# First two expert-query slots split by token halves inside the second norm, and three remainders made on Pool: one edit to a one-core decoder-layer kernel

## The reference, cut to what matters

```
h = layernorm(alpha * h + cross_attention(h))          # the "second norm"
q = h @ peer_wq          # 2048 x 2048: the expert queries
s = q . sub_keys         # per head and half, 128 keys; then top-16 and the experts
```

## Time and profile before

| | |
|---|---|
| time, median of 3 runs | 1891.31 us (1889.75 to 1891.76) |
| the profiled execution's own time | 1890.53 us |
| its span | 1888.8 us |
| PE busy | 98% of the span |
| DVE, ACT, POOL busy | 77%, 45%, 18% |
| the stretch of the change | from about 512 to 540 us of the span |

### The profile page before, as it was taken

One profiled execution on the slowest core, in us unless ns is written; L12 is line 12 of the kernel. 1 busy time (PEld: TensorE's weight loads), 2 busy tenths in 40 slices (PEclk: granted clock), 3 DMA queues, 4 the chain that ended last, 5 costly groups with the idle time before them and its releaser, 6 DMA issues.

```text
span 1888.8 us, 25810 instructions
## 1 busy us (share of the span) xinstructions
PE 1852.9 (98%) x10392; PEld 1625.5 (86%) x10392; DVE 1459.4 (77%) x1917; ACT 841.4 (45%) x1136; POOL 345.4 (18%) x216
## 2 busy tenths in 40 slices
PE   7999999999899999999999999999999999999997
PEld 6888888888688999999777889889889899898895
DVE  6544655576763798996888888888988988989886
ACT  5443456344533101223555545455455455454552
POOL 1000223000000001001333223222323223323200
PEclk9999999999989999999999999999999999999999
DMA  9645433746254777888999999999999999999881
GB/s 343 240 178 178 136 133 120 320 162 245 90 201 156 245 268 282 329 325 318 358 370 366 359 361 362 390 352 371 385 350 379 376 353 391 363 355 393 349 314 45
DMA packets 100199, 548.21 MB, mean 290 GB/s; under 512 B 8705, under 2 KB 33345, under 8 KB 35953
## 3 DMA queue, kind: packets, MB, share of 16 engines
q1 hardware_dynamic: 53424, 374.37, 52.2%
q0 software_dynamic: 20096, 147.04, 19.2%
q10 hardware_dynamic: 26560, 25.17, 4.3%
HBM read 530.74 MB, written 14.68 MB: 289 GB/s over the span
## 4 chain that ended last, share of the span: by engine, by line
PE 96%; DVE 1%; ACT 1%; DMA 1%; issue 1%; SPq 0%; POOL 0%; DVEq 0%; ACTq 0%
PE bank L947 15%; PE bank L849 11%; PE bank L575 11%; PE bank L592 9%; PE bank L949 7%; PE bank L880 6%; PE bank L883 6%; PE bank L881 6%; PE bank L879 6%; PE bank L882 6%; PE bank L577 5%; PE bank L869 2%; PE bank L815 1%; DMA ring_raw<-in_stream 1%; PE bank L682 0%
## 5 line engine op out<-in xcount | busy, mean ns | idle before, releaser
L575 PE MATMUL bank<-act_split,ring_hi 128*128 128x512 f32 x896 | 319.4, 400 | 10.9 <-DVE ring_lo L1355 8.2
L1816 DVE TENSOR_TENSOR split_a<-experts,split_a 128x2048 fp32r<-128x2048 f32 x120 | 274.6, 2289 | 53.1 <-ACT split_a L1270 52.8
L1344 DVE TENSOR_TENSOR ring_lo<-ring_raw,ring_hi 128x2048 fp32r<-128x2048 f32 x90 | 205.9, 2290 | 137.3 <-ACT ring_hi L1010 136.9
L1270 ACT CAST split_a<-experts 128x2048 fp32r<-128x2048 f32 x120 | 229.7, 1914 | 140.5 <-PE bank L883 139.7
L947 PE MATMUL bank<-h_split,split_a 128*128 128x384 f32 x944 | 270.8, 359 | 0.0
L577 PE MATMUL bank<-act_split,ring_lo 128*128 128x256 f32 x896 | 251.9, 281 | 0.0
L949 PE MATMUL bank<-h_split,split_a 128*128 128x192 f32 x944 | 236.3, 250 | 0.0
L549 POOL DMA_INDIRECT rows<-in_peer_u,eidx x64 | 139.9, 2186 | 448.9 <-DVE rows L1723 443.0
L549 POOL DMA_INDIRECT rows<-in_peer_v,eidx x64 | 153.0, 2391 | 368.4 <-DVE hrow L1729 344.7
L849 PE MATMUL bank<-h2T,experts 128*128 128x192 f32 x1280 | 216.3, 326 | 0.0
L575 PEld LDWEIGHTS bank<-act_split,ring_hi 128*128 128x128 f32 x896 | 169.7, 189 | 50.4 <-DVE act_split L1355 8.0
(11 more groups left out here) (277 smaller groups left out, 3422.5 us busy)
## 6 DMA issues: line engine op xcount, KB each, us to landing
experts<-in_stream SPq DMA_DIRECT2D x221, 1024.0 KB, 7.4
ring_raw<-in_stream SPq DMA_DIRECT2D x91, 1024.0 KB, 4.8
late_raw<-in_stream SPq DMA_DIRECT2D x35, 1024.0 KB, 7.9
gate_matrix<-stage ACTq DMA_DIRECT2D x12, 1024.0 KB, 4.9
gbuf<-gate_matrix ACTq DMA_DIRECT2D x16, 768.0 KB, 12.9
w<-in_w SPq DMA_DIRECT2D x4, 1024.0 KB, 8.7
gb<-in_ln_g POOLq DMA_DIRECT2D x3, 1024.0 KB, 4.8
gb<-in_ln_b POOLq DMA_DIRECT2D x3, 1024.0 KB, 9.2
```

The source lines that it names most:

```text
L575: pe.matmul(bank[n % 2][:, :], hi[:, k * P:(k + 1) * P], act_split[:, k].rearrange("p c t -> p (c t)"), start=(k == 0), stop=False, skip_g ...
L1270: act.copy(split(m)[0], tile).then_inc(split_hi, 1)
L1344: dve.tensor_tensor(ring_lo[:, r, :], ring_raw[:, r, :], ring_hi[:, r, :].bitcast(F32), ALU.subtract).then_inc(lo_ready, 1)
L1816: dve.tensor_tensor(lo, raw_slot(split_slot(m))[0], hi.bitcast(F32), ALU.subtract).then_inc(split_lo, 1)
```

## The change

Four edits, in one stretch.

1. PE: the first two query slots are done by token halves. `half_slot(b, t, q)` does 4 of the 16 `k` steps of slot b for the 128 tokens of half t: a matmul of 2 x 128 columns with the slot's high part and one of 128 columns with its low part. The order is: turn t=0, slots 0 and 1 for t=0, turn t=1, slots 0 and 1 for t=1, and then `block_slot` for the other 14 slots.
2. ACT: the four copies to the high part come first, and the whole copies to `h2T` after the low parts.
3. DVE: all four `half_low` of t=0 come before the first `scaled` of t=1, mixed with two `centred`, and the four of t=1 after the norm.
4. POOL makes the low parts of the second to fourth slot (three subtractions of 128 x 2048), which DVE made after its last `half_low`. The turned tiles go to other banks.

```diff
--- before.py
+++ after.py
@@ -520,6 +520,11 @@
                 for j, name in enumerate((f"ln{k + 1}_g", f"ln{k + 1}_b")):
                     pool.dma_start(gb[:, j, :], a[name].partition_broadcast(P)).then_inc(gb_landed, 16)
 
+            pool.wait_ge(lo_ready, S_PQ + 1)
+            for s in range(S_PQ + 1, S_PQ + R):
+                pool.wait_ge(hi_ready, s + 1)
+                pool.tensor_tensor(ring_lo[:, s % R, :], ring_raw[:, s % R, :], ring_hi[:, s % R, :].bitcast(F32),
+                                   ALU.subtract).then_inc(lo_ready, 1)
             pool.wait_ge(ln_ready, 16)
             pool.wait_ge(slots_done, S_PQ + 1)
             pool.dma_start(subk[:], a["subkT"]).then_inc(subk_landed, 16)
@@ -816,17 +821,49 @@
                                              ring[w][:, r, i * 512:(i + 1) * 512], start=(i == 0 and n == 0),
                                              stop=(i == 3 and n == 2))
                     last.then_inc(slots_done if t else xo_first, 1)
-            for t in range(TT):
+            def turn_half(t, q):
+                pe.wait_ge(ln_ready, 8 + 4 * t + q + 1)
+                if t and q >= 2:
+                    pe.wait_ge(act_lo, A_XO + q - 1)
+                    pe.wait_ge(h2_ready, q - 1)
+                for i in range(4):
+                    k = 4 * q + i
+                    last = pe.transpose(bank[PQ_BANKS[t][q]][:, i * P:(i + 1) * P], hres[:, t, k * P:(k + 1) * P], ident[:])
+                last.then_inc(ht_done, 1)
+            def half_slot(b, t, q):
+                out = bank[(N_PQ + b) % 2]
+                if q == 0 and t == 0:
+                    pe.wait_ge(lo_ready, S_PQ + b + 1)
+                    pe.wait_ge(dve_nb, 8 + 4 + XO_BANKS[1].index((N_PQ + b) % 2) + 1)
+                if b == 0:
+                    pe.wait_ge(act_lo, A_XO + 4 * t + q + 1)
+                hi, lo = (pq_first[:, w] if b == 0 else ring[w][:, (S_PQ + b) % R] for w in range(2))
+                tokens = slice(t * P, (t + 1) * P)
+                for k in range(4 * q, 4 * q + 4):
+                    pe.matmul(out[:].rearrange("p (c t) -> p c t", c=2)[:, :, tokens], hi[:, k * P:(k + 1) * P],
+                              act_split[:, k, :, tokens], start=(t == 0 and k == 0), stop=False, skip_group_check=True)
+                    last = pe.matmul(out[:, tokens], lo[:, k * P:(k + 1) * P], actT_hi[:, k, tokens], start=False,
+                                     stop=(k == KO - 1), skip_group_check=True)
+                if t and q == 3:
+                    last.then_inc(slots_done, 1)
+            for q in range(4):
+                turn_half(0, q)
+            for q in range(4):
+                half_slot(0, 0, q)
+            for q in range(4):
+                half_slot(1, 0, q)
+            for q in range(4):
+                turn_half(1, q)
+            for b in range(2):
                 for q in range(4):
-                    pe.wait_ge(ln_ready, 8 + 4 * t + q + 1)
-                    for i in range(4):
-                        k = 4 * q + i
-                        last = pe.transpose(bank[XO_BANKS[t][q]][:, i * P:(i + 1) * P], hres[:, t, k * P:(k + 1) * P], ident[:])
-                    last.then_inc(ht_done, 1)
-
-            for b in range(16):
+                    half_slot(b, 1, q)
+            for b in range(2, 16):
                 pe.wait_ge(tb_out, N_PQ + b - 1)
-                block_slot(S_PQ + b, N_PQ + b, fresh=[A_XO + n for n in HALF_LOW] if b == 0 else None)
+                block_slot(S_PQ + b, N_PQ + b)
 
             pe.wait_ge(tb_out, N_U)
             pe.wait_ge(dve_nb, 16)
@@ -1199,21 +1236,28 @@
             for b in range(1, 4):
                 high(S_PQ + b)
 
+            def turned(t, q):
+                return bank[PQ_BANKS[t][q]][:].rearrange("p (k t) -> p k t", k=4)
             def turned_high(t, q):
+                act.wait_ge(ht_done, 8 + 4 * t + q + 1)
+                act.copy(actT_hi[:, 4 * q:4 * q + 4, t * P:(t + 1) * P], turned(t, q)).then_inc(act_hi, 1)
+            def turned_whole(t, q):
                 n = (P, ND - P)[t]
-                act.wait_ge(ht_done, 8 + 4 * t + q + 1)
-                turned = bank[XO_BANKS[t][q]][:].rearrange("p (k t) -> p k t", k=4)
-                act.copy(actT_hi[:, 4 * q:4 * q + 4, t * P:(t + 1) * P], turned).then_inc(act_hi, 1)
-                act.copy(h2T[:, 4 * q:4 * q + 4, t * P:t * P + n], turned[:, :, 0:n]).then_inc(h2_ready, 1)
+                act.wait_ge(act_lo, A_XO + 4 * t + q + 1)
+                act.copy(h2T[:, 4 * q:4 * q + 4, t * P:t * P + n], turned(t, q)[:, :, 0:n]).then_inc(h2_ready, 1)
 
             act.wait_ge(slots_done, S_PQ)
-            turned_high(0, 0)
-            turned_high(0, 1)
+            for q in range(4):
+                turned_high(0, q)
             deviation(3, slice(1, 2))
-            turned_high(0, 2)
-            turned_high(0, 3)
+            for q in range(4):
+                turned_whole(0, q)
             for q in range(4):
                 turned_high(1, q)
+            for q in range(4):
+                turned_whole(1, q)
             for b in range(16):
                 if b and b + AHEAD < 16:
                     high(S_PQ + b + AHEAD)
@@ -1648,10 +1692,9 @@
             def half_low(t, q):
 
                 dve.wait_ge(act_hi, A_XO + 4 * t + q + 1)
-                dve.wait_ge(h2_ready, 4 * t + q + 1)
                 sl = (slice(None), slice(4 * q, 4 * q + 4), slice(t * P, (t + 1) * P))
                 part((actT_hi[sl], actT_lo[sl]),
-                     bank[XO_BANKS[t][q]][:].rearrange("p (k t) -> p k t", k=4)).then_inc(act_lo, 1)
+                     bank[PQ_BANKS[t][q]][:].rearrange("p (k t) -> p k t", k=4)).then_inc(act_lo, 1)
 
             low(S_XO + 3)
             add_half(0, 0)
@@ -1668,24 +1711,20 @@
                     marks.append(centred(0, j + 2, gb))
             for j in range(1, NQ):
                 add_half(1, j)
+            half_low(0, 0)
             half_variance(1)
-            half_low(0, 0)
             half_low(0, 1)
-            marks = [centred(1, j, gb) for j in range(2)]
-            scaled(1, 0, gb, marks[0], 3)
+            marks = [centred(1, 0, gb)]
             half_low(0, 2)
-            scaled(1, 1, gb, marks[1], 3)
-            marks.append(centred(1, 2, gb))
-            half_low(1, 0)
-            scaled(1, 2, gb, marks[2], 3)
-            marks.append(centred(1, 3, gb))
-            half_low(1, 1)
-            scaled(1, 3, gb, marks[3], 3)
+            marks.append(centred(1, 1, gb))
             half_low(0, 3)
-            half_low(1, 2)
-            half_low(1, 3)
-            for b in range(1, R):
-                low(S_PQ + b)
+            for j in range(NQ):
+                scaled(1, j, gb, marks[j], 3)
+                if j + 2 < NQ:
+                    marks.append(centred(1, j + 2, gb))
+            for q in range(4):
+                half_low(1, q)
+            dve.wait_ge(lo_ready, S_PQ + R)
             for b in range(16):
                 block_sum(N_PQ + b, pq[:, b, :])
                 if b + R < 16:
@@ -1927,7 +1966,7 @@
 HT_BANKS = ((6, 7), (2, 3))
 HEAD_QUARTERS = (0, 2, 1, 3)
 XO_BANKS = ((2, 3, 4, 5), (1, 0, 6, 7))
-HALF_LOW = (4, 5, 7, 8)
+PQ_BANKS = ((2, 3, 4, 5), (6, 7, 2, 3))
 V0_BANKS = (2, 3, 0, 1)
 V0_FIRST = (0, 1, 2, 3)
 V0_LAST = (3, 2, 0, 1)
```

## The result

The changed kernel takes 1896.42 us (median of 8 runs, 1894.77 to 1898.31), the kernel before 1891.2 in the same comparison (8 runs, 1887.35 to 1892.6): a ratio of 1.0027, 95% interval 1.0018 to 1.0036. It is **slower by 0.27%**, 5.2 us. The forecast of 1885.8 had the wrong sign; the rival "DVE waits behind POOL" named 1898. The stated range, 1884.2 to 1897.5, holds 1896.42 only because it was drawn around gain and loss.

The account below looks back on a forecast made before the run. PE, busy for 98% of the span, was taken as the bound. Slot 2 5.6 us earlier, carried in full from 1890.5, gives 1884.9; with 0.8 for the median 1885.7, stated as 1885.8, range 1884.2 to 1897.5.

Parts of the forecast that it names:

- DVE waits behind POOL: Rival: `scaled` operations of t=0 wait for POOL's subtractions, DVE 10.8 us late, 6.7 us slower overall, 1898; chance 0.30.
- POOL's three subtractions: Slots 1 to 3's low parts on POOL: 5.4 us each, 7.0 available, so no cost if engines don't hamper each other.
- The rest (clock, less gaps): Rival's term for PE's long gap: 2.7 us lost to the clock's fall less 1.2 of gaps, 1.5 us.
- The time of 1896: The POOL-wait rival reckoned with 4497 ns per POOL operation instead of 5.4 us: DVE delay 9, time 1896.
- The half steps: PE's steps in slots 0 and 1 by token halves: 0.225 us each, bounds 0.173 and 0.28.
- PE's new timeline: PE from turning t=0 to slot 2: slot 2 starts at 533.9 instead of 539.54, 5.6 us earlier.
- DVE's order: DVE's reordered low parts and norm: quarters may start from 516.2, norm of t=1 done at 524.0 instead of 525.1.
- DVE's three `ring_lo`: DVE's three subtractions, 6.7 us, lay under slot 0; without the move to POOL they would be a cost.
- ACT's order: ACT's same eight casts and eight copies in another order: costs nothing.
- Carrying it to the end: Slots 2 to 15 and the rest are PE's chain, so the 5.6 us gain reaches the end in full.
- the second rival: Clock falls in PE's gaps (1 to 2.5 us) or half steps are dear (3 us): about 1888; chance 0.14.
- dear half steps: Case in slots 0 and 1: half steps take 0.28 us each, costing 3 us of the gain.

Follow-up runs that it names:

- pool_timed: Changed kernel with POOL's first subtraction after the norm of t=0, the others after that of t=1, DVE's wait after the first block sum: 1888.03 us.
- pool_alone: Kernel before the change with only POOL's three subtractions moved over from DVE, whole slots kept: 1900.62 us.
- pool_memset: Changed kernel with POOL's three subtractions replaced by memsets to zero, so POOL only writes: 1887.83 us.
- pool_one_input: Changed kernel with POOL's three subtractions replaced by a one-input multiplication by zero in the same places: 1896.13 us.
- lows_on_dve: Changed kernel with POOL's three subtractions given back to DVE, behind its last low parts of t=0 and t=1: 1887.64 us.
- pool_timed_again: The kernel pool_timed unchanged, run once more for a second profile: 1888.34 us.
- pool_alone_timed: Kernel pool_alone with POOL's subtractions held back until the norm of t=1 is done, DVE's wait behind the first block sum: 1891.82 us.
- before: The kernel without the change, the reference: 1891.2 us.
- experiment 8: Changed kernel with each of POOL's three subtractions cut into eight pieces of 128 x 256, in the same places: 1890.39 us.
- after: The changed kernel with all four edits, against the kernel before: 1896.42 us.
- after_again: The changed kernel unchanged, run once more for a second profile: 1896.27 us.

## Why the prediction was wrong

**The step that failed** is that of POOL's three subtractions: "this costs nothing if the engines don't hamper each other". They do, and its price is the whole of the loss: 8.6 us of DVE, where the sum had 0. Take that hold away and the same work gains (pool_timed). The rows at hand said both things. Rows 8 showed POOL shut out for a whole operation by a DVE subtraction, and the Trainium skill ("SBUF — State Buffer", Who interferes with whom) says that the order of issue decides which of the two is blocked; rows 9 showed an overlap without it, and I gave rows 9 the greater weight. Rows 9 had operations of 128 and 256 columns with one input; the change has 2048 columns and two. pool_alone, pool_timed and pool_memset show that the exclusion is there at this size and that POOL's reading makes it; pool_one_input shows that the one input alone does not excuse it. Extending a row to eight times its length and another operand count was the mistake. The same page of the Trainium skill ("SBUF — State Buffer", Summary: rules for kernel authors) has the second of the two wait until the first finishes. With two inputs on POOL the trace agrees (5.09 against 0.75); with one input the hold is there but ends about 1.7 before POOL's end, where the measurement decides.

**The rival that came true** had the place and the number of waits right: two, at `scaled` operations of t=0, and a third operation that passes under the additions. One of its terms was clearly too dear: POOL's operation is 4.58 by itself and 4.94 to 5.00 where it first waits for a DVE operation to end, instead of 5.4, so that the delay is 8.6, not 10.8. The rest (clock, less gaps) was put at 1.5 and is what is left over: 30.58 − 26.75 + 5.5 − 8.6 = 0.7 in the first profiles, 1.4 with the means of two profiles of each kernel (31.2 − 26.1 + 4.9 − 8.6). So the rival's +6.7 becomes 8.6 − 5.5 + 0.7 = +3.8, or 8.6 − 4.9 + 1.4 = +5.1, where the medians say +5.2. The Trainium skill ("GPSIMD Engine Reference", Performance versus the Vector engine) gives 4497 ns for a two-input `tensor_tensor` (an addition) of this size; the trace has 4.58 for the subtraction. The time of 1896 that the prediction worked out with that figure is the nearest to the 1896.42 measured.

**What was right.** *The half steps:* 0.225 forecast, 0.23 measured (544.07 to 544.30). *PE's new timeline:* 5.6 us earlier at slot 2, measured in pool_timed as 26.75 − 21.23 = 5.5, with PE's first half step 3.5 after the first turning (forecast: 3.4) and the clock at 1.00 throughout, as forecast (so it was in lows_on_dve and pool_timed_again too, but not in pool_memset). *DVE's order:* with nobody in the way its operations come as the sum had them: in pool_timed from the last statistics of t=1 (518.66) to the end of its norm (527.65) pass 9.0 us; from 514.79 to the forecast 524.0 it was 9.2. *DVE's three `ring_lo`* lay under slot 0, so that it brings nothing to take them off DVE (pool_alone_timed). *ACT's order* showed no cost: in lows_on_dve PE's first half step also comes 3.5 after the first turning.

**Carrying it to the end** was a bit too good. The profile before that the sum was made against had 13.7 us of low clock in the stretch; in a second one it was 10.2, and the gain against that is smaller by 1.3. A slow pace of the full slots takes another 1.4 in some executions. And what lies ahead of the stretch varies as well: the spans of the two profiles differ by only 1.6 (1888.8 and 1887.2), since pool_timed's stretch begins 3.9 later, behind 10.2 us of low clock where before had 3.4. So 5.5 in the one profile is 2.5 us in the median of pool_timed, with an interval of 1.5 to 5.1. The number of the second rival, 1888, is what lows_on_dve and pool_timed give. Its dear half steps didn't come, and in the three profiles of these two kernels the clock didn't fall; in pool_memset it did, and slot 2 came 2.6 later. How much of the shortfall of the medians is such falls in executions without a profile is not shown.

## What to carry to other kernels

Before an elementwise operation goes to POOL, list which DVE instructions run beside it: those with two SBUF inputs are each held to POOL's end (5 us for 128 x 2048 with two inputs), those with a PSUM input or one input are not. Put POOL's part beside the latter, or cut it in pieces, and look at the duration of single instructions, since the hold counts as busy time. And when two rows disagree about an interference, list what each lacks of the case at hand (length, number of inputs, who comes first): neither rows 8 nor rows 9 had a long two-input operation on POOL, so neither could settle it. Ask first whether the operation moved was on the path at all: here it was not.

## What the runs showed of the hardware that was not expected

**POOL gets in behind every instruction.** In the changed kernel POOL's second operation starts at 516.02 while a `scaled` finishes its delayed work (to 516.61), and the next `scaled`, from 516.53, is held until POOL has ended. DVE's list had instructions ready all the time. The pieces of experiment 8 show the same turn-taking ten times.

**One input isn't cheaper on POOL.** 128 x 2048 takes 5.35 with one SBUF input (a multiplication by a constant), where the two-input subtraction takes 4.58; writing alone takes 1.81.

**Two paces of the full slots.** Slots 2 to 15 take 77.9 us in pool_timed and 79.35 in pool_timed_again (stretch less "to slot 2" in the table), the same kernel, both at full clock: 0.347 or 0.353 a step. after and after_again differ in the same way, and 5 of the 14 profiles have the slower pace. All 5 are among the 10 with half slots; the 4 with whole slots have the faster one. That may be chance, or a cost of the half slots that the sum didn't have; no run was made for it, and what decides it stays open.

**The clock's low spells are not the kernel's alone.** A spell of 3.4 or 6.8 us near 140 us of the span, before anything that was changed, is in 13 of the 14 profiles and not in the first one of before; it and its neighbours move the beginning of the stretch between 512.4 and 516.7. This and the two paces set how far a stretch read in one profile can stand from a median: 1 to 3 us.
